# Three more pairs of gate products in the seven-product form, and the sums they need begun earlier

## What is computed

```python
h = rmsnorm(x, g_pre)
proj = h @ w_in                       # 12 parts of 512 columns and 4 x 1024 gate logits
v_n = layernorm(a_v)                  # chunk mixing of branch a uses v_n
out_a, out_b, out_c, out_d = ...      # four branches, each 512 wide
                                      # branch b: 31-tap causal convolution over tokens
gates = sigmoid(gate_logits + b_gate)           # four gates of 1024 channels
merged = sum(gates[n] * (out_n @ w_branch[n]) for n in range(4))
x = x + rmsnorm(merged @ w_out, g_post)
```

## Time and profile before

| | us |
|---|---|
| median of 3 runs (2425.59 to 2429.27) | 2427.77 |
| the profiled execution, its own time | 2427.47 |
| its span (first to last instruction) | 2425.5 |
| PE busy / weight loads busy | 2400.0 / 2080.0 |
| DVE busy | 1459.1 |
| POOL busy / ACT busy | 568.9 / 442.8 |

### The profile page before, as it was taken

How to read it: one execution, slowest core, us unless ns; L and a number is a source line. 1 busy time by engine, 2 the same in 40 slices (tenths; PEclk the granted TensorE clock), 3 DMA queues, 4 the chain that set the end, 5 groups by cost and what they waited for, 6 DMA issues and landing times.

```text
span 2425.5 us, 32867 instructions
## 1 busy us (share of the span) xinstructions
PE 2400.0 (99%) x12520; PEld 2080.0 (86%) x12520; DVE 1459.1 (60%) x2088; ACT 442.8 (18%) x660; POOL 568.9 (23%) x304
## 2 busy tenths in 40 slices
PE   9999999999999999999999999999999999999997
PEld 7888887788888888788888888878899999999997
DVE  7776877752456556754256656764336676577643
ACT  5222222323011111121102111111200111011111
POOL 5435444454022223212112222313100000000000
PEclk9999999999999999999999999999999999999999
DMA  8868887786765877766666787856674437988877
GB/s 333 316 236 298 305 290 280 257 297 257 256 256 217 311 265 299 277 230 256 226 242 238 265 302 275 305 207 257 234 245 163 142 139 259 330 280 266 286 263 274
DMA packets 165548, 632.57 MB, mean 261 GB/s; under 512 B 14832, under 2 KB 17264, under 8 KB 119344
## 3 DMA queue, kind: packets, MB, share of 16 engines
q1 hardware_dynamic: 151184, 606.03, 69.7%
q10 hardware_dynamic: 14240, 24.89, 2.9%
HBM read 466.70 MB, written 164.16 MB: 260 GB/s over the span
## 4 chain that ended last, share of the span: by engine, by line
PE 95%; DVE 2%; issue 1%; DMA 1%; ACT 0%; POOL 0%; DVEq 0%; POOLq 0%; SPq 0%; ACTq 0%
PE acc L1642 69%; PE acc L1855 8%; PE acc L1970 6%; PE side L1782 4%; PE side L1866 3%; PE side L1855 2%; PE acc L1747 1%; PE side L1809 1%; PE side L1799 1%; DMA w_pair<-split_main 0%; PE side L1667 0%; DVE cb L1008 0%; DVE tmp L1251 0%; PE acc L1788 0%; DMA xr<-in_x_t 0%
## 5 line engine op out<-in xcount | busy, mean ns | idle before, releaser
L1642 PE MATMUL acc<-h_hi,w_pair 128*128 128x512 f32 (+1 forms) x4576 | 1304.7, 370 | 0.0
L1642 PEld LDWEIGHTS acc<-h_hi,w_pair 128*128 128x128 f32 x4576 | 818.4, 188 | 142.6 <-issue 3.6
L1642 PE MATMUL acc<-h_lo,w_pair 128*128 128x512 f32 (+1 forms) x2288 | 800.7, 368 | 0.0
L1642 PEld LDWEIGHTS acc<-h_lo,w_pair 128*128 128x128 f32 x2288 | 415.8, 188 | 71.9 <-issue 3.6
L1008 DVE SCALAR_TENSOR_TENSOR cb<-glu,col,cb 128x512 f32<-128x512 f32 x600 | 440.7, 800 | 22.0 <-issue 15.4
L519 POOL TENSOR_TENSOR w_pair<-w_raw,w_pair 128x1024 fp32r<-128x1024 f32 x118 | 269.5, 2296 | 278.5 <-ACT w_pair L645 263.3
L1642 PE MATMUL acc<-out_hi,w_pair 128*128 128x512 f32 (+1 forms) x896 | 277.5, 378 | 8.7 <-DVE tmp L1251 8.7
L552 POOL TENSOR_TENSOR rstd<-msq,nhalf 128x5 f32<-128x5 f32 (+3 forms) x18 | 19.2, 1067 | 815.9 <-DVE msq L936 564.4
L1642 PEld LDWEIGHTS acc<-out_hi,w_pair 128*128 128x128 f32 x896 | 164.1, 189 | 41.1 <-DVE tmp L1251 10.8
L707 ACT ACTIVATE sig<-acc,col 128x512 f32<-128x512 f32 (+1 forms) x104 | 72.2, 694 | 659.9 <-PE acc L1642 657.9
L543 POOL TENSOR_TENSOR s_lo<-w_raw,s_hi 128x1024 fp32r<-128x1024 f32 x44 | 113.3, 2598 | 231.9 <-ACT s_hi L656 231.9
(11 more groups left out here) (246 smaller groups left out, 2764.4 us busy)
## 6 DMA issues: line engine op xcount, KB each, us to landing
w_pair<-split_main SPq DMA_DIRECT2D x228, 1024.0 KB, 4.9
split_main<-w_pair SPq DMA_DIRECT2D x88, 1024.0 KB, 6.8
w_raw<-in_w_main SPq DMA_DIRECT2D x132, 512.0 KB, 5.7
chunk<-s_parts SPq DMA_DIRECT2D x88, 512.0 KB, 5.9
w_pair<-split_branch SPq DMA_DIRECT2D x72, 512.0 KB, 3.9
chunk<-split_main SPq DMA_DIRECT2D x66, 512.0 KB, 5.8
s_parts<-s_hi SPq DMA_DIRECT2D x22, 1024.0 KB, 4.0
s_parts<-s_lo SPq DMA_DIRECT2D x22, 1024.0 KB, 7.0
```

The costliest lines, as they stand in the source:

```text
L1642: ins = pe.matmul(acc[:, s, b, 0:m], wt[slot][:, wk], mv_[:, k, t0:t0 + m], start=(k == 0 and n == 0), stop=(k == nk - 1 and n == 2))
```

## The change

The first gate section of the last block, G0, keeps its first two gates as units; its other six gates become three pairs, ahead of the pairs of D (25 pairs in all). The run of pairs begins at `SEVEN_AT`, the fifth unit of G0. Weight sums are needed for three pairs more: `SUM_AT` gets the rounds 0 and 2, in sections B and V of blocks 1 and 2; block 2 no longer has one at round 26. The activation sums are made from the mixing section on, and in front of the first gate's multiplication. The convolution's taps are dealt out anew.

```diff
-SEVEN = [("D", 8), ("G1", 4), ("G2", 4), ("Z", 2), ("G3", 4)]
+SEVEN = [("G0", 3), ("D", 8), ("G1", 4), ("G2", 4), ("Z", 2), ("G3", 4)]
...
+SEVEN_AT = UNIT0["G0"] + 4
...
-SUM_AT = [4, 6, 8, 10, 12, 14, 16, 18, 20, 24, 26]
+SUM_AT = [0, 2, 4, 6, 8, 10, 12, 14, 16, 18, 20, 24, 26]
...
+                q0 = (j - 1) * len(SUM_AT)
+                if name in ("B", "V") and 0 < j < NBLK - 1:
+                    s_pair_sums(q0 + (name == "V"))
                 if name in ("B", "C", "O"):
                     for r in range(count):
...
                 if last:
-                    conv_step(j, 8 + i)
+                    conv_step(j, 8 + 2 * i)
+                    conv_step(j, 9 + 2 * i)
...
                 if last:
-                    conv_step(j, 10 + c)
+                    conv_step(j, 12 + c)
+                    if c in (1, 2):
+                        t_sums(*{1: ((1, 0), (1, 1)), 2: ((1, 2),)}[c])
...
-            merge(0, 0, 4, conv_at=14 if last else 6)
+            if last:
+                t_sums((2, 0), (2, 1), (3, 0), (3, 1), (3, 2))
+                t_low(1)
+                merge(0, 0, 1, after={0: lambda: t_sums((4, 0), (4, 1)), 1: lambda: [t_low(t) for t in (2, 3, 4)]})
+            else:
+                merge(0, 0, 4, conv_at=6)
...
             if last:
+                dve.drain()
+                for q in range(3):
+                    pair_sums(q)
+                    for t in range(2):
+                        conv_step(j, 16 + 2 * q + t)
+                        seven_merge(q, t)
                 for i in range(CT):
                     seven_d(i)
...
-            gated(0, 0, 4)
             if last:
+                gated(0, 0, 1)
                 seven_pairs()
             else:
+                gated(0, 0, 4)
                 section(j, "D", 0, 4, body4)
```

More of the change, by code:

```diff
@@ L507, in body @@
                             split_load(u, r + turn, src, n)
-                for i in range(count // 4):
+                for i in range(1 if j == NBLK - 1 and name == "G0" else count // 4):
                     body(i)
+                if j == NBLK - 1 and name == "G0":
+                    sp.wait_ge(s_stored, 32 * NPAIR)
+                    for p in range(NPAIR):
+                        load_pair(p)
         for r in range(KT):
@@ L836, in body @@
                                 s_cast(j, UNIT0[name] // 4 + i, r)
-                    if last and name == "G0":
-                        t_cast(i)
+                if last:
+                    act.wait_ge(v_stored, 16)
+                    t_cast(1)
+                    body(0)
+                    for t in (2, 3, 4):
+                        t_cast(t)
+                    return
                 if n > 1:
@@ L1201, in _, with t_sums, t_low @@
                 if last:
-                    conv_step(j, 8 + i)
+                    conv_step(j, 8 + 2 * i)
+                    conv_step(j, 9 + 2 * i)
+            def t_sums(*steps):
+                ht = [[f(h)[:, c0:c0 + CT, s:s + HALF] for h in (h_hi, h_lo)]
+                      for c0, s in ((0, 0), (0, HALF), (CT, 0), (CT, HALF))]
+                b11, b12, b21, b22 = ht
+                terms = {1: (b12[0], b11[0], b12[1], b11[1]), 2: (b22[0], t_sum[1], b22[1]),
+                         3: (b22[0], b12[0], b22[1], b12[1]), 4: (b21[0], t_sum[2], b21[1])}
+                for t, n in steps:
+                    x, y, *more = terms[t]
+                    dve.drain()
+                    if n == 0:
+                        ins = dve.tensor_tensor(t_sum[t][:, :, :], x, y, ALU.subtract)
+                    else:
+                        ins = dve.tensor_tensor(t_sum[t][:, :, :], t_sum[t][:, :, :], more[n - 1],
+                                                ALU.add if n == 1 else ALU.subtract)
+                    if n == len(more):
+                        ins.then_inc(t_summed, 1)
+            def t_low(t):
+                dve.wait_ge(t_hi_done, t)
+                dve.tensor_tensor(t_lo[t][:, :, :], t_sum[t][:, :, :], f(t_hi[t])[:, :, :],
+                                  ALU.subtract).then_inc(t_lo_done, 1)
             for c in range(CT):
@@ L1231, in _, with merge @@
             wn = width(min(j + 1, NBLK - 1))
-            def merge(ph, start, end, conv_at=None):
+            def merge(ph, start, end, conv_at=None, after=()):
                 u0 = ub + UNIT0[f"G{ph}"]
@@ L1269, in body @@
                         dve.drain()
-                        if last and ph == 0:
-                            t_steps(m)
+                        if after and m in after:
+                            after[m]()
                         if conv_at is not None:
@@ L1886, in seven_pairs @@
                     bank = banks(p)
[L1887 removed]
+                    same = (name, q) != ("G1", 0) and (name != "D" or q == 0)
                     if p == 0:
```

114 lines of the change are left out of this document (45 added, 69 removed).

## The result

| | us |
|---|---|
| before, median of 21 runs (2425.59 to 2429.34) | 2427.31 |
| changed, median of 21 runs (2428.93 to 2433.94) | 2430.92 |
| ratio, with its 95% interval | 1.0014 (1.0007 to 1.0020) |
| profiled execution: before / changed | 2427.47 / 2430.09 |
| its span: before / changed | 2425.5 / 2428.3 |

The changed kernel is slower by 0.14%, 3.4 us. That is inside the 0.2% taken as the bound, and the forecast of 2430.9 stands beside a median of 2430.92. That the two agree to the hundredth is luck: the forecast started from a median of 2427.8 of three runs, where 21 runs give 2427.31, and its sum was +3.1 where the two medians are 3.6 apart. The sum has to be looked at term by term, since errors in it can have cancelled.

What follows compares the result with a forecast made beforehand. PE was taken as the bound, busy 99% of the span. The terms -5.1 + 4.3 + 0.7 + 1.6 + 1.6 = +3.1 us on the profiled 2427.47 gave 2430.6, forecast as a median of 2430.9; range 2426 to 2435.

Steps and rivals of the forecast that it cites:

- three pairs: G0, last block: a pair costs PE 17.53 us against 19.24 as two units; three save 5.1 us.
- stall for the first `merged`: G0, last block: PE waits before the second branch unit for DVE's late first gate multiplication, 4.3 us (4.0 to 4.6).
- wait for the low part of sum 2: G0's first pair: after its first product PE waits for DVE's low part of sum 2, 0.7 us.
- half clock behind the stall: Behind G0's stall: one stretch at 1.2 GHz, costing 1.6 us; from nothing to 3.2 us.
- the two row jobs: Section B, blocks 1 and 2: POOL's power, behind weight sums, makes PE's row job wait 0.8 us each, 1.6 together.
- load in O: Section O: three first loads issued one or two chunks later; costed at nothing, half a microsecond if cover is gone.
- block 2's half clock: Block 2, behind PE's 2.2 us wait: clock 0.50 from 1591.3 to 1594.7 before; the sum has no term for it.
- Rival 1: G0: the clock doesn't fall behind the stall; sum +1.5, 2429.3 us; chance 0.12.
- Rival 2: Section B, blocks 1 and 2: POOL's sums hold up DVE; +4.9 to +6.5, 2432.7 to 2434.3 us; chance 0.2.
- Rival 3: G0: DVE catches up before the first gate, no stall or half clock; -3.5 to -5.1, 2424.3 to 2422.7; chance 0.1.

Runs made afterwards that it cites:

- the best: Changed kernel with two taps moved from M into G0's pairs, sum 2's low part before the second gate's multiplication, block 2 without round 20: 2420.47 us, ratio 0.9970.
- the kernel with the sums alone: Kernel before, still 22 pairs, with only the weight sums begun in sections B and V of blocks 1 and 2: 2424.48 us, ratio 0.9987.

## Why the prediction was right, point by point

| term | predicted | measured | by |
|---|---|---|---|
| three pairs | -5.1 | -4.9 | PE's lag behind the kernel before, 6.9 at the first pair and 2.0 at the end of G0 |
| stall for the first `merged` | 4.3 | 4.33 | its wait; 0.7 and 7.9 with a tap less and more |
| wait for the low part of sum 2 | 0.7 | 0.9 | its wait; gone when its instruction moved |
| half clock behind the stall | 1.6 | 2.3 | 5.50 against 3.2 us |
| the two row jobs | 1.6 | 0.8 | PE's lateness against before, 0.4 at each |
| load in O | 0 (0.5 if bare) | 0.5 | its wait, 0.7 for 0.2 |
| block 2's half clock | unchanged | -1.6 | 1.00 for 0.50 at 1591 |

The measured column adds up to +2.3; the profiled spans differ by 2.8. Most of the half microsecond between them can be located: the changed kernel's first matmuls in the chain start 0.1 us late (14.54 for 14.44), and 0.3 us come at the very end, where 24.40 us lie between the last power and what follows it in the chain, for 24.07. Why they do is open.

**The stall** is right in place, cause and size. The whole of it lies 0.7 to 0.8 us earlier than the prediction's clock times, with PE, since block 2 lost its half clock. One reading there is loose: the 0.26 us called the only idle time of DVE from 1947.31 on are the only wait for PE; with the small gaps between instructions DVE is idle for 1.7 of those 18.4 us. The sum is not touched, since its round and its sums were taken from start to start.

**The low part of sum 2** is right, and 0.2 too small. Half clock is not the reason, since the wait is 0.9 with one and two taps out too, where there is none. The joints are: from the end of the branch unit to that of the low part it is 2.4 us (1980.33 to 1982.74) for the 2.3 worked out, and PE's first product starts 0.2 us ahead of that end, at 1980.16.

**The clock** is right in that it falls and in place; the size was taken from 3.4 us of half clock and there were 6.8, of which a third lay in the stall. The upper bound of 3.2 holds. Behind the same stall of 4.3 us the branch unit took 5.50 us in the changed kernel, 5.71 with the power first and 4.85 with round 20 left out, so the cost was 2.3, 2.5 and 1.6 in three executions: the 1.6 of the forecast is the low end. What the prediction had not thought of is that half clock could go elsewhere. In the twelve profiled executions it came behind all four stalls of 4.3 us or more that G0 had (3.4 us with round 20 left out, 6.8 in the changed kernel and with the power first, 10.2 with one tap more). Behind block 0's wait of 2.0 us, which every kernel has, it came in six of the twelve, and behind block 2's of 2.2 us in three of the eight that have it: before, and the two with the power first and round 20 kept. In two executions, one tap out and the best, it came at neither place and not in G0. (All twelve also have 12.6 to 14.9 us of half clock at their very end, the kernel before too, 13.8.) So one execution tells little of a term of 1.6 us, and the medians of many runs are needed for it. What decides which of the short waits is followed by half clock stays open.

**The row jobs** are the term that was mis-sized: 2 x 0.8 predicted, 2 x 0.4 measured, just under even the low end of 0.5. Within the block the power is late by 2.06 us, where 2.2 to 2.7 was worked out; from its end to `diag_lo`'s end it takes 1.8 as read in the earlier trace rows. The step that failed is the choice of 0.8 from 0.5 to 1.0 "since DVE's own small copies get in between POOL's instructions here": it was the copy that was held up, to 1.10 us, and POOL's two low parts took the 4.74 us of a quiet place.

**The load in O** is not settled. It is 0.4 us in the kernel with the sums alone, which has the old ring of chunks, and 0.3 to 1.1 in the others. The change of `TURN` is not shown to be its cause.

**Rival 1** (the clock stays) did not happen behind any of the four profiled stalls of 4.3 us or more. **Rival 2** (POOL holds up DVE in B): the tiles landed at 1212.03, two microseconds later than worked out and one before the 1213 from which it decides, and two residual additions of 0.69 us took 0.82 and 1.03; DVE then waited 4.03 us for PE where it had waited 4.51. The mechanism is there, at a tenth of the price that would have made it count. **Rival 3** (the gain arrives) did not happen, as the round did not get shorter (1956.76 - 1946.59 = 10.17 us, with 1.43 of it the sum that was added); it is what the moved taps bring.

Two errors cancelled: the row jobs, 0.8 too much, stand against the clock's 0.7 too little. The load in O and block 2's clock lay outside the sum, +0.5 and, in the executions where it is so, -1.6. So the mechanism and the large terms were right, and the closeness of the total is in part luck.

## What to carry to other kernels

When a bound engine's queue gets shorter by some microseconds, add up the other engine's chain from the last point where it still waits, and compare it with the moment at which its result is asked for: here that gave the stall to a tenth, and moving 3.6 us pieces of work to the far side of that moment turned a loss of 0.14% into a gain of 0.18%. Look at the waits that are there already before adding new work: the 2.2 us one in block 2 came from POOL reading SBUF beside DVE's two-input instructions, and one pair of sums at another round gave back 2.9 us, more than the 1.7 that a pair of gates saves. And look at what the moved work will stand beside, not only what it stood in front of.

## What was unexpected of the hardware

- A DVE instruction of 0.17 us for four elements per partition took 1.25 us when it started 0.07 us after a POOL instruction of 1.29. In block 0 of the kernel before the same cast takes 2.36 us, begun 0.06 us after a POOL instruction of 2.40:

```profile
439.62 2.36 DVE L948 CAST rstd_hi<-rstd 128x4 fp32r<-128x4 f32 x1 [6.75 <-POOL rstd L552]
```

  What is lost goes by the neighbour's length, not by the instruction's own. The chain goes on from this cast to the multiplication for which PE stands 2.0 us at 444.50, the wait of block 0 that every kernel here has; an estimate from these rows is that nearly all of it would go with those 2.2 us, but no run tried it. The cast has one input, and was held up all the same; the section of the Trainium skill named above has casts among the instructions that can take the shared ports, in a two-port mode.
- Twelve instructions of the convolution's taps in section V, 8.4 us in the kernel before, took 12.66 beside POOL's two low parts (5.29 us). It lay off the path there; the same loss in G2 of block 2 was on it.
- Half clock inside the kernel lasted 3.4 us, 6.8 and 10.2 in different executions, behind waits of 2.0 to 7.9 us, and came behind a wait of 2.0 us in some executions and not in others. It also ran on after PE was at work again: with one tap more until 1985.45, 5.3 us after the branch unit had begun.
